# A transformer layer on one core: two normalisations whose results are multiplied piece by piece, with other pieces and another order on VectorE and TensorE

## The reference

```python
def _layernorm(x, g, b):
    xf = x.astype(jnp.float32)
    mu = jnp.mean(xf, -1, keepdims=True)
    var = jnp.mean(jnp.square(xf - mu), -1, keepdims=True)
    return ((xf - mu) * lax.rsqrt(var + LN_EPS) * g + b).astype(x.dtype)
...
    h = _layernorm(ALPHA * x + 0.5 * _swiglu(x, p['ffa_w_gu'], p['ffa_w_down']),
                   p['ln1_g'], p['ln1_b'])
    proj = h @ p['w_in']
...
    h = _layernorm(ALPHA * h + mix, p['ln2_g'], p['ln2_b'])
    y = _layernorm(ALPHA * h + 0.5 * _swiglu(h, p['ffb_w_gu'], p['ffb_w_down']),
                   p['ln3_g'], p['ln3_b'])
```

## Time and profile before

| | us |
|---|---|
| median of 3 executions | 1314.1 |
| lowest, highest | 1307.41, 1315.0 |
| the profiled execution's own time | 1313.7 |
| its span in the profile | 1311.7 |

### The profile page before, as it was taken

One profiled execution on the slowest core, in us unless ns is written; L12 is line 12 of the kernel. 1 busy time (PEld: TensorE's weight loads), 2 busy tenths in 40 slices (PEclk: granted clock), 3 DMA queues, 4 the chain that ended last, 5 costly groups with the idle time before them and its releaser, 6 DMA issues.

```text
span 1311.7 us, 30883 instructions
## 1 busy us (share of the span) xinstructions
PE 1258.7 (96%) x13254; PEld 1139.8 (87%) x13254; DVE 561.8 (43%) x851; ACT 422.5 (32%) x678; POOL 89.2 (7%) x89
## 2 busy tenths in 40 slices
PE   9999999999999999997879988899999999999996
PEld 8999999999999988885447544698999999999996
DVE  4333332323437444345543644687533333323353
ACT  4222222222324324333433334333422222222222
POOL 0000000000100110000450012010000000000021
PEclk9999999999999999999997999999999999999997
DMA  6222222222223757645643889741322222222221
GB/s 227 96 96 93 73 90 96 68 89 89 89 85 113 270 197 236 228 134 184 227 150 105 282 283 297 256 175 51 112 81 80 94 96 96 80 65 89 89 65 65
DMA packets 57846, 176.95 MB, mean 135 GB/s; under 512 B 7313, under 2 KB 7570, under 8 KB 49426
## 3 DMA queue, kind: packets, MB, share of 16 engines
q1 hardware_dynamic: 54578, 169.48, 38.7%
q10 hardware_dynamic: 3168, 6.02, 1.3%
HBM read 164.64 MB, written 10.83 MB: 134 GB/s over the span
## 4 chain that ended last, share of the span: by engine, by line
PE 87%; DVE 5%; issue 2%; ACT 2%; DMA 1%; SPq 1%; POOL 1%; DVEq 0%; ACTq 0%; POOLq 0%
PE acc L298 66%; PE acc L854 3%; PE acc L1611 2%; PE acc L1681 2%; PE acc L321 1%; PE acc L1164 1%; PE acc L1876 1%; PE acc L1868 1%; PE acc L545 1%; PE acc L1853 1%; PE acc L424 1%; PE acc L1843 1%; PE acc L1956 1%; PE acc L1188 1%; PE acc L411 1%
## 5 line engine op out<-in xcount | busy, mean ns | idle before, releaser
L279 DVE TENSOR_TENSOR weights_lo<-weights_raw,weights_hi 128x1024 fp32r<-128x1024 f32 (+2 forms) x184 | 206.7, 1125 | 518.9 <-ACT weights_hi L272 518.9
L272 ACT ACTIVATE weights_hi<-weights_raw 128x1024 fp32r<-128x1024 f32 (+2 forms) x184 | 177.5, 966 | 539.3 <-PE acc L298 518.2
L298 PE MATMUL acc<-x_hi,weights_hi 128*128 128x260 f32 x1696 | 344.6, 284 | 0.6 <-DVE weights_lo L264 0.5
L298 PE MATMUL acc<-x_hi,weights_lo 128*128 128x260 f32 x1696 | 342.0, 283 | 0.0
L298 PE MATMUL acc<-x_lo,weights_hi 128*128 128x260 f32 x1696 | 341.6, 283 | 0.0
L298 PEld LDWEIGHTS acc<-x_hi,weights_hi 128*128 128x128 f32 x1696 | 261.9, 189 | 13.7 <-issue 11.7
L298 PEld LDWEIGHTS acc<-x_hi,weights_lo 128*128 128x128 f32 x1696 | 261.8, 189 | 0.0
L298 PEld LDWEIGHTS acc<-x_lo,weights_hi 128*128 128x128 f32 x1696 | 261.0, 188 | 0.0
L298 PE MATMUL acc<-hidden_hi,weights_hi 128*128 128x260 f32 x684 | 139.2, 285 | 0.0
L298 PE MATMUL acc<-hidden_hi,weights_lo 128*128 128x260 f32 x684 | 137.8, 283 | 0.0
L298 PE MATMUL acc<-hidden_lo,weights_hi 128*128 128x260 f32 x684 | 137.7, 283 | 0.0
(11 more groups left out here) (348 smaller groups left out, 1367.3 us busy)
## 6 DMA issues: line engine op xcount, KB each, us to landing
cache_pages<-in_cache_k SPq DMA_DIRECT2D x128, 256.0 KB, 3.6
weights_raw<-in_gate_up_b SPq DMA_DIRECT2D x22, 1024.0 KB, 4.9
weights_raw<-in_gate_up_a SPq DMA_DIRECT2D x21, 1024.0 KB, 4.8
cache_pages<-in_cache_v SPq DMA_DIRECT2D x64, 256.0 KB, 3.6
weights_raw<-in_w_in SPq DMA_DIRECT2D x13, 1024.0 KB, 6.2
projected<-in_cache_v SPq DMA_DIRECT2D x48, 256.0 KB, 3.6
weights_raw<-in_down_a SPq DMA_DIRECT2D x8, 768.0 KB, 4.1
weights_raw<-in_down_b SPq DMA_DIRECT2D x8, 768.0 KB, 4.2
```

Of the source, the lines that this page charges most:

```text
L272: nc.scalar.activation(WH[pr.slot(k)][:, 0:nk, :], RAW[slot][:, 0:nk, P * (k % 2):P * (k % 2) + P], ACT.Copy).then_inc(split_hi, 1)
L279: nc.vector.tensor_tensor(WL[pr.slot(k)][:, 0:nk, :], RAW[slot][:, 0:nk, P * (k % 2):P * (k % 2) + P], WH[pr.slot(k)][:, 0:nk, :].bitcast( ...
L298: mm = nc.tensor.matmul(acc[s][:, a, 0:HALF], w[slot][:, t, :], x[:, k0 + t, HALF * a:HALF * a + HALF], start=begins and t == tiles[0] and ...
```

## The change

Norms 0 and 1 get the ten pieces that the last norm has: only chunks 0 and 1 in halves, chunk 2 whole. On DVE each low part comes one piece later in the order, and the variance, the scale and the inverse of the second half come ahead of the first low part. On ACT the copy of the spread inverse's second half comes ahead of the third piece's x_hi. On PE both spreads of the second half stand behind the high pairs of the first piece, and each piece's low products come behind the next piece's high pairs. Chunk 2 is multiplied by three slabs at once, behind the wait for its low part, and slab 3 follows with chunks 0, 1 and 2. The computation is the same.

```diff
-        PARTS = ((0, 0), (1, 0), (2, 0), (0, 1), (1, 1), (2, 1), (3, None), (4, None), (5, None), (6, None), (7, None))
-        LAST_PARTS = ((0, 0), (1, 0), (0, 1), (1, 1), (2, None), (3, None), (4, None), (5, None), (6, None), (7, None))
+        PARTS = ((0, 0), (1, 0), (0, 1), (1, 1), (2, None), (3, None), (4, None), (5, None), (6, None), (7, None))
...
             shift_out_scalar(act, n, 1)
-            biased_scalar(act, n, 2)
             if following:
                 inverse_out_scalar(act, n, 1)
-            for e in range(3, len(PARTS if following else LAST_PARTS)):
+            biased_scalar(act, n, 2)
+            for e in range(3, len(PARTS)):
                 biased_scalar(act, n, e)
                 if following and e == 4:
                     split_high(act, following, 0, 3)
...
             shift_sub_vector(dve, n, 1, 0)
-            low_part(dve, n, 0)
             variance_vector(dve, n, 1)
             scale_vector(dve, n, 1)
             inverse_vector(dve, n, 1)
+            low_part(dve, n, 0)
+            shift_sub_vector(dve, n, 0, 1)
             low_part(dve, n, 1)
-            shift_sub_vector(dve, n, 2, 0)
             for e in range(2, len(PARTS)):
                 scale_vector(dve, n, e)
+                if e > 2:
+                    low_part(dve, n, e - 1)
                 if e + 1 < len(PARTS):
                     shift_sub_vector(dve, n, *PARTS[e + 1])
-                low_part(dve, n, e)
-                if e == 5:
+                if e == 4:
                     split_low(dve, following, 0, 3)
+            low_part(dve, n, len(PARTS) - 1)
...
-            for e in range(6):
+            for e in range(4):
                 c, h = PARTS[e]
-                pe.wait_ge(x_hi, DC + 11 * n + e + 1)
+                pe.wait_ge(x_hi, DC + 10 * n + e + 1)
                 for k in first:
                     high(k, c, h)
-                    if e == 0 and k == first[1]:
-                        shift_spread_tensor(pe, n, 1)
-                if e == 1:
+                if e == 0:
+                    shift_spread_tensor(pe, n, 1)
                     inverse_spread_tensor(pe, n, 1)
-                pe.wait_ge(x_ready, DC + 11 * n + e + 1)
-                for k in first:
-                    matmul(k, c, h, 2)
-            for c, h in PARTS[:6]:
+                if e:
+                    pe.wait_ge(x_ready, DC + 10 * n + e)
+                    for k in first:
+                        matmul(k, *PARTS[e - 1], 2)
+            pe.wait_ge(x_ready, DC + 10 * n + 4)
+            for k in first:
+                matmul(k, *PARTS[3], 2)
+            pe.wait_ge(x_ready, DC + 10 * n + 5)
+            for k in first:
+                for h in range(2):
+                    high(k, 2, h)
+                    matmul(k, 2, h, 2)
+            for c, h in ((0, 0), (1, 0), (0, 1), (1, 1), (2, 0), (2, 1)):
                 high(3, c, h)
                 matmul(3, c, h, 2)
             for c in (3, 4, 5):
-                pe.wait_ge(x_ready, DC + 11 * n + c + 4)
+                pe.wait_ge(x_ready, DC + 10 * n + c + 3)
```

More of the change, by code:

```diff
@@ L682, in norm_pool @@
                 elif n:
-                    pool.wait_ge(scaled, 11 * n)
+                    pool.wait_ge(scaled, 10 * n)
                 pool.tensor_tensor(SCR[:, 5, :], Y[:, 0, :] if c == 1 else SCR[:, 5, :], Y[:, c, :], ALU.add)\
@@ L724, in biased_scalar @@
         def biased_scalar(act, n, e):
-            c, h = (LAST_PARTS if n == 2 else PARTS)[e]
-            act.wait_ge(scaled, 11 * n + e + 1)
+            c, h = PARTS[e]
+            act.wait_ge(scaled, 10 * n + e + 1)
             bias = VEC[:, V_LN + (2 * n + 1) * DC + c:V_LN + (2 * n + 1) * DC + c + 1]
@@ L771, in scale_vector @@
         def scale_vector(dve, n, e):
-            c, h = (LAST_PARTS if n == 2 else PARTS)[e]
+            c, h = PARTS[e]
             if n < 2:
-                dve.wait_ge(g("shift_taken"), 11 * n + e + 1)
+                dve.wait_ge(g("shift_taken"), 10 * n + e + 1)
             elif (c, h) in LAST_TAKEN:
-                dve.wait_ge(g("shift_taken"), 11 * n + LAST_TAKEN.index((c, h)) + 1)
+                dve.wait_ge(g("shift_taken"), 10 * n + LAST_TAKEN.index((c, h)) + 1)
             else:
@@ L796, in low_part @@
             b = V_LN + (2 * n + 1) * DC + c
-            dve.wait_ge(x_hi, DC + 11 * n + e + 1)
+            dve.wait_ge(x_hi, DC + 10 * n + e + 1)
             nc.vector.scalar_tensor_tensor(out=piece(XL, c, h), in0=piece(Y, c, h), scalar=VEC[:, b:b + 1],
@@ L2720, in _ @@
             sp.dma_start(TABLE[:, :], pages).then_inc(g("table_in"), 16)
-            sp.wait_ge(x_ready, DC + 11)
+            sp.wait_ge(x_ready, DC + 10)
             sp.dma_start(Y[:, 0:2, :], consts[:, NCONST + NLATE:NCONST + NLATE + 2 * TOK].rearrange("p (a n) -> p a n", n=TOK))\
@@ L2772, in _ @@
             for c in range(DC):
-                sp.wait_ge(x_hi, DC + 22 + c + 3)
+                sp.wait_ge(x_hi, DC + 20 + c + 3)
                 sp.dma_start(y_out[:, c, :], Y[:, c, :]).then_inc(stored, 16)
```

## The result

The changed kernel takes 1317.1 us in the median of 20 executions (1312.2 to 1327.1), the kernel before 1309.6 us in 20 run beside it (1302.7 to 1317.2). The ratio is 1.0059 with a 95% interval of 1.0040 to 1.0077. By the ratio the change costs 7.7 us, between 5.2 and 10.1, which is less than 1%; the two medians lie 7.5 apart. The profiled execution took 1316.32 us with a span of 1314.5, against 1313.7 and 1311.7 before.

A forecast was written before the change was run, and what follows sets the result against it. PE was taken to bound the kernel, with 87% of the 1311.7 us chain. Per norm, 2.9 us of stalls plus 1.7 of low clock, twice, made 9.2 us; on 1314.1 that gave 1323 us, range 1315 to 1329.

The forecast's parts named there:

- PE bounds it and only the two stretches matter: First products behind norms 0 and 1: time is decided where PE waits; at most 4.2 us to win.
- Variance and inverse first, no effect: DVE, half 1's variance and inverse ahead of the first low part (done at about 400.25): costs and gains nothing.
- Both spreads earlier: PE, both spreads behind the first piece: second halves start 1.05 us earlier, the change's real gain.
- Pieces 2 and 3: Second halves of chunks 0 and 1: PE waits 0.75 us for x_hi, then 0.37 for a low part.
- Chunk 2 behind the weight split: Chunk 2's low part queues on DVE behind slab 3's weights_lo: PE stalls 3.56 us, stretch +2.9 us per norm.
- The clock: PE's clock falls in both norms after the long stall: 3.4 us low, costing 1.7 us per norm, bounds 0 and 6.8.
- longer than either gap: Clock argument: the 3.56 us stall exceeds earlier PE idle times of 2.70 (clock fell) and 1.65 us (held).
- A: Rival, norm stretches: same stalls, clock stays up in one or both; +5.8 to +7.5 us, about 1320.5; chance 0.27.
- B: Rival, norm stretches: clock falls and stays down; 9.7 us per norm, together 19.4, 1333.5 us; chance 0.08.
- C: Rival, chunk 2: its low part doesn't wait behind weights_lo, so the gain arrives; 1310 to 1313 us; chance 0.06.
- D: Rival, mixing stage: cache-page loads running ahead give back norm 0's delay; about +4.6 left, 1318.7 us; chance 0.07.

The follow-up runs named there:

- experiment 1: Three edits of the changed kernel: low_first, split_later, and one without the low parts' one-piece lag; ratios to before 1.0003, 1.0007 and 1.0003.
- low_first: Changed kernel with chunk 2's low part on DVE ahead of slab 3's weights_lo and chunk 3's scale; ratio to before 1.0003.
- split_later: Changed kernel with slab 3's weights_lo one piece later on DVE, behind chunk 2's low part; ratio to before 1.0007.
- spreads_only: Kernel before with only both second-half spreads behind the first piece and ACT's inverse copy ahead of the third piece's x_hi; ratio 0.9988.
- keep_busy: Changed kernel with 28 extra 260-column matmuls on PE where it waits for chunk 2's low part; ratio to before 1.0015.

## Why the prediction was right, point by point

The forecast was 9.2 us slower; measured are 7.7, with 9.2 inside the interval of 5.2 to 10.1, and the six stretches make 9.2. The forecast of the time itself, 1323 us, came out 5.9 too high, at 1317.1, only 2.1 above the lower end of its range. 4.5 us of that are not the change's: the base was a median of three, 1314.1, and the 20 executions beside the changed kernel give 1309.6.

- *PE bounds it and only the two stretches matter.* Right within what the runs resolve: the fixes of experiment 1, all within them, bring the ratio back to 1.0003 to 1.0007, with intervals of about 0.003 to each side.
- *Variance and inverse first, no effect.* As said: first low part at 399.88, nobody waits for it.
- *Both spreads earlier.* The inverse's second half is read at 401.51 on ACT, 1.0 us earlier than at 402.51 before. Right for the changed kernel. Taken alone the part gains 0.3 us per norm.
- *Pieces 2 and 3.* Waits of 0.69 and 0.32 in the rows of the weight loads where I had 0.75 and 0.37 between starts.
- *Chunk 2 behind the weight split.* The low part was set at 408.67 to 409.43 and ran 408.72 to 409.48 (the whole execution is 0.08 us late from 398.43 on), the wait at 3.56 between starts, 3.50 as the engine's idle time. low_first and split_later show both of its halves. With the clock held the stretch is 29.81, where 26.94 + 2.87 was forecast as +2.9.
- *The clock.* The step was a choice on the length of the wait, and it held in six stretches of six. Its size is 1.75 us on average against 1.7, which is luck in part, since errors cancel. The low time is 3.4 us four times and 6.8 twice; of the 6.8, 1.75 lie in the wait and cost nothing; and dense products of 260 columns lose 45% of the low time and not half, since at the upper level they go 0.120 us apart and at the lower 0.217, while the spreads of the earlier trace rows really double. The argument behind the step was too simple, and the trace before already said so. It has a second long idle time that the prediction didn't name, 2.79 us to 688.27, and there the clock fell as well; but it held behind 1.86 us to 824.63, and it fell at 707.9 with no idle time over 0.95 us in the 6 us before. In the runs split_later's clock fell after a wait of 1.66 us, spreads_only's behind 1.00 and 0.27. So "longer than either gap" gave the right answer for waits of 3.5 us and can't be used as a rule.
- *Rivals.* A, the clock stays up, is out (none in six), and keep_busy is what it would have looked like. B is out: no low stretch behind the wait is longer than 6.8 us, half of the 13.7 that B took. C is out, the low part waits behind the weights_lo as the order says. D, the delay given back in the mixing stage, had the first profile's span for it. As a whole it is out, since its +4.6 us lie below the interval of 5.2 to 10.1, and the stage's own clock explains that span. A part of it may be true: the 1.5 us between 9.2 and 7.7 are within chance, and no run tests the loads that D names.

## What to carry to other kernels

When a step is put "one piece behind", read what stands between on its engine at the seams: here the lag of one piece alone made a wait of 1.66 us, and the one instruction that was not part of the pattern, a weight split that itself waited for another engine, made it 3.5. Let a consumer wait only for what it uses next, the high part first and the low part behind its products. And where chance of the clock moves the total by more than the edit, compare the stretch between two fixed instructions over several profiles rather than the span of one.

## What the runs showed of the hardware

- The granted clock fell while PE was hardly idle: in spreads_only at about 399.1, behind waits of 1.00 and 0.27 us, and it was 0.50 from 400 to 404 with PE busy throughout; in split_later once in two stretches, after one wait of 1.66 us. In the 13 other stretches of kernels with both spreads in a row and no wait over 1.00 us it held.
- Behind the same wait of 3.5 us the clock fell in six stretches of six, but not at the same moment: from 1.75 us before the wait ended to 0.7 us into the products behind it.
- At the lower level products of 260 columns go 0.217 us apart (21 steps from 409.91 to 414.46 in the changed kernel) against 0.120 at the upper, a factor of 1.8; the 16 matmuls of the spreads take 3.53 against 1.87, 1.9.
- The mixing stage spent between 3 and 34 us at the lower clock in 13 profiles of nearly the same program. Over 35 executions of the kernel before, the time at the lower clock goes with most of the spread of the times (correlation 0.89).
